# Moving the sample rows' top-k rounds from the delta stage back into the last projections

## The reference, cut to what matters

```python
# sparse attention: the indexer's score, and the keys that it leaves
score = jnp.einsum('bqh,bqhk->bqk', iw, jax.nn.relu(dots))     # 8 index heads
_, idx = lax.top_k(score, n_top)        # prompt 128 of 512 keys, sample rows 68 of 272
...
# delta rule, per chunk of 64: decay from cumulative gates, triangular solve, state
decay = jnp.exp(jnp.where(tri, gc[..., :, None] - gc[..., None, :], -jnp.inf))
sol = lax.linalg.triangular_solve(a, rhs, left_side=True, lower=True, unit_diagonal=True)
```

## Time and profile before

| | |
|---|---|
| median of 3 runs | 1534.19 us |
| the profiled execution's own time | 1533.19 us |
| its span, first to last instruction | 1531.4 us |
| PE busy | 1449.6 us, 95% |
| DVE busy | 883.3 us, 58% |
| mean granted TensorE clock | 0.977 |
| end of the projections, start of the delta stage | about 809 us into the span |

### The profile page before, as it was taken

One profiled execution on the slowest core, in us unless ns is written; L12 is line 12 of the kernel. 1 busy time (PEld: TensorE's weight loads), 2 busy tenths in 40 slices (PEclk: granted clock), 3 DMA queues, 4 the chain that ended last, 5 costly groups with the idle time before them and its releaser, 6 DMA issues. The chain is left out here.

```text
span 1531.4 us, 28524 instructions
## 1 busy us (share of the span) xinstructions
PE 1449.6 (95%) x11426; PEld 1351.3 (88%) x11430; DVE 883.3 (58%) x1637; ACT 573.9 (37%) x1130; POOL 394.7 (26%) x360
## 2 busy tenths in 40 slices
PE   6899999999999989998998889998999999999996
PEld 3889999999999989988896668688899999999995
DVE  2636665575477451576565766563557458754863
ACT  2632332342243252653324423542544124422443
POOL 1702420331242240541002030112723024302400
PEclk9899999999999989999999999999999999999998
DMA  9424445445443323222106020233113312331221
GB/s 344 130 83 139 152 132 172 138 145 165 131 139 100 96 57 78 78 69 62 50 1 160 2 88 16 71 100 87 56 42 97 97 56 84 96 98 48 83 77 69
DMA packets 211736, 148.76 MB, mean 97 GB/s; under 512 B 18075, under 2 KB 190396, under 8 KB 211608
## 3 DMA queue, kind: packets, MB, share of 16 engines
q1 hardware_dynamic: 206264, 129.15, 28.8%
q0 software_dynamic: 5344, 17.81, 3.7%
HBM read 139.99 MB, written 6.95 MB: 96 GB/s over the span
## 5 line engine op out<-in xcount | busy, mean ns | idle before, releaser
L1005 PE MATMUL pair<-b_hi,w_hi 128*128 128x320 f32 x720 | 224.3, 312 | 0.0
L1005 PE MATMUL pair<-b_hi,w_lo 128*128 128x320 f32 x720 | 222.5, 309 | 0.0
L1005 PE MATMUL pair<-b_lo,w_hi 128*128 128x320 f32 x720 | 222.4, 309 | 0.0
L1075 PE MATMUL pair<-act_hi,w_hi 128*128 128x320 f32 x704 | 161.9, 311 | 0.0
L1075 PE MATMUL pair<-act_hi,w_lo 128*128 128x320 f32 x704 | 160.4, 309 | 0.0
L1075 PE MATMUL pair<-act_lo,w_hi 128*128 128x320 f32 x704 | 160.4, 309 | 0.0
L471 DVE SCALAR_TENSOR_TENSOR x_t<-pair,gate,x_t 128x320 f32<-128x320 f32 (+1 forms) x128 | 56.0, 479 | 167.5 <-PE pair L1075 142.1
L1005 PEld LDWEIGHTS pair<-b_hi,w_hi 128*128 128x128 f32 x720 | 135.1, 188 | 14.3 <-DVE w_lo L594 8.4
L588 ACT ACTIVATE w_hi<-sums_a 128x512 fp32r<-128x512 f32 x72 | 45.1, 627 | 251.9 <-POOL sums_a L622 132.0
L890 DVE TENSOR_TENSOR uvw<-pair,uvw 128x320 f32<-128x320 f32 (+1 forms) x126 | 67.6, 537 | 123.1 <-PE pair L1005 122.7
L1005 PEld LDWEIGHTS pair<-b_lo,w_hi 128*128 128x128 f32 x720 | 135.2, 188 | 0.0
(11 more groups left out here) (428 smaller groups left out, 3160.2 us busy)
## 6 DMA issues: line engine op xcount, KB each, us to landing
w_mod_raw<-w_mod SPq DMA_DIRECT2D x28, 1024.0 KB, 6.0
w_raw<-ffn_w_gate SPq DMA_DIRECT2D x40, 512.0 KB, 4.1
raw_more<-ffn_w_up SPq DMA_DIRECT2D x40, 512.0 KB, 3.8
w_raw<-w_in SPq DMA_DIRECT2D x24, 512.0 KB, 3.7
w_raw<-ffn_w_down SPq DMA_DIRECT2D x16, 384.0 KB, 3.3
raw_more<-ffn_w_down SPq DMA_DIRECT2D x16, 384.0 KB, 3.1
w_mod_a<-w_mod POOLq DMA_DIRECT2D x4, 1024.0 KB, 10.9
w_mod_b<-w_mod POOLq DMA_DIRECT2D x4, 1024.0 KB, 24.1
```

Source lines behind the costliest of these rows:

```text
L1005: mm = pe.matmul(job_bank(j, BANK_OF[part]), w[:, at, kk], mv[:, kk, s], start=(kk == 0 and v == 0 and part in FIRST_OF_BANK), stop=(kk == ...
L1075: mm = pe.matmul(pair[part % 2][:, b, 0:HALF], w[:, slot, k], mv[:, k, b * HALF:(b + 1) * HALF], start=(k == 0 and v == 0), stop=(k == n - ...
```

## The change

The sample job becomes an ordinary fourth job of `next_rounds`. Its scores are copied at its first round, now into the score buffer. It may start once v is at least 25, so that it comes behind the third job: 6 rounds at the end of v = 28, and the last 2, the partial round and the mask at the end of v = 29. All calls of `sample_rounds` and `sample_mask` in the delta stage go. SP, ahead of the bias rows, and ACT, ahead of the first exponential, now wait for the fifth mask instead of the fourth. PE's waits are as they were.

```diff
@@ mix_loads (SP), and exps (ACT) with the same edit
-            sp.wait_ge(S["mask"], 4)
+            sp.wait_ge(S["mask"], 5)
@@ mix_dve
-            score_s = v_f[:, TOK - LS:]
...
+                first = left[job] == TOPK_S // 8
                 left[job] -= n
                 final = not left[job]
-                s = score_of(job)
+                s = score[:, SCORE_AT[job]:SCORE_AT[job] + SCORE_N[job]]
+                if job == 3 and first:
+                    dve.wait_ge(S["sscore"], NB)
+                    dve.tensor_copy(s, bank[3][:, 0:LS]).then_inc(S["sscore_out"], 1)
+                    dve.wait_ge(S["sscore_out"], 1)
                 topk(job, n, at)
-                if final and job < 3:
+                if job == 3 and final and TOPK_S % 8:
+
+                    link(dve.max(mx[:], s))
+                    link(dve.memset(mx[:, TOPK_S % 8:], NEG_TAKEN))
+                    link(dve.match_replace(s, mx[:], s, NEG_TAKEN))
+                if final:
                     make_mask(job)
...
-                if v >= SCORE_V + IDX_HEADS // PER_STEP and any(left[0:3]):
+                if v >= SCORE_V + IDX_HEADS // PER_STEP and (any(left[0:3]) or any(left) and v >= SAMPLE_V + NB // 2):
                     next_rounds(2 if v <= V["g", 11] else 1 if v <= V["aq", 1] else 6)
-            while any(left[0:3]):
+            while any(left):
                 next_rounds(4)
-            sample_scores()
@@ delta_dve, levels of the sample tile, and level 1
-                sample_rounds(1 if lv else 2)
...
-            sample_rounds(2)
-            level(1, 0, both((sample_rounds, 1), (w_out, 0)))
+            level(1, 0, lambda: w_out(0))
             level(1, 1, None, place_own)
-            level(1, 2, both((sample_mask,), (new_v, 0)))
+            level(1, 2, lambda: new_v(0))
```

More of the change, by code:

```diff
@@ L1765, in exps @@
                 if j == 0:
-                    act.wait_ge(S["mask"], 4)
+                    act.wait_ge(S["mask"], 5)
                     act.wait_ge(S["sscore"], NB)
@@ L1822, in mix_dve @@
             link = chained(dve, S["chain"])
-            score_s = v_f[:, TOK - LS:]
-            def score_of(job):
-                return score[:, SCORE_AT[job]:SCORE_AT[job] + SCORE_N[job]] if job < 3 else score_s
             def topk(job, n, before):
-                s = score_of(job)
+                s = score[:, SCORE_AT[job]:SCORE_AT[job] + SCORE_N[job]]
                 with dve.Fori(0, n) as i:
@@ L1856, in next_rounds @@
                 at = sum((ROUNDS,) * job) + (ROUNDS if job < 3 else TOPK_S // 8) - left[job]
+                first = left[job] == TOPK_S // 8
                 left[job] -= n
                 final = not left[job]
-                s = score_of(job)
-                topk(job, n, at)
-                if final and job < 3:
-                    make_mask(job)
[L1864 to L1875, removed]
+                s = score[:, SCORE_AT[job]:SCORE_AT[job] + SCORE_N[job]]
+                if job == 3 and first:
+                    dve.wait_ge(S["sscore"], NB)
+                    dve.tensor_copy(s, bank[3][:, 0:LS]).then_inc(S["sscore_out"], 1)
+                    dve.wait_ge(S["sscore_out"], 1)
+                topk(job, n, at)
+                if job == 3 and final and TOPK_S % 8:
[3 more added lines that the diff above has]
+                if final:
+                    make_mask(job)
             def place_v(h, part):
@@ L2003, in mix_dve @@
             dve.wait_ge(S["cols"], 1)
-            delta_dve(dve, link, next_rounds, sample_mask, *attention_dve(dve, link))
+            delta_dve(dve, link, *attention_dve(dve, link))
             dve.wait_ge(S["st_out"], 16)
@@ L2011, in mix_dve, with delta_dve @@
                 add_to_x(dve, 1, U_OUT + m, m, X_OUT + m, U_OUT + m + 2)
-        def delta_dve(dve, link, sample_rounds, sample_mask, biased, normed, place_own):
+        def delta_dve(dve, link, biased, normed, place_own):
             def matrices(q):
```

## The result

| | before | after |
|---|---|---|
| median, comparison of the change (6 runs each) | 1534.08 us (1533.19 to 1534.84) | 1543.19 us (1541.0 to 1546.8) |
| median, compared once more (`e1_again`) | 1535.05 us (30 runs, 1533.14 to 1541.12) | 1540.74 us (11 runs, 1538.35 to 1544.5) |
| the profiled execution: time, span, mean granted clock | 1533.19, 1531.4, 0.977 | 1539.34, 1537.5, 0.977 |

The change makes the kernel slower: the ratio is 1.006, with an interval of 1.0048 to 1.0073, and 1.004 (1.0027 to 1.0053) the second time. The sign and the place of the first delay are as forecast. The median of 1543.19 us is 4.5 us above the forecast of 1538.7, and 0.7 us above the end of its range; the second one, 1540.74 us, lies inside the range. Beside its six runs the first comparison has two more executions of the kernel after, of 1539.34 us (the profiled one) and 1543.66 us.

The account below looks back on a forecast made before the run. PE, busy for 95% of the span, was taken to bound the kernel. Terms 7.8 - 0.5 - 1.5 + 0.65 = 6.4 us, less 2.6 times about three quarters, gave 4.5 us: 1538.7 us forecast, range 1535.7 to 1542.5.

Parts of the forecast that it names:

- Steps 1 and 2: Border of projection and delta stage: DVE gets 13.65 us more, 5.64 us of cover, `matrices(0)` 7.8 us late at 818.9.
- Step 3: From `matrices(0)` to `k_in`: 0.60 us of waiting for PE falls away, `k_in` 7.3 us late at 822.3.
- step 4: First L2018 against POOL: up to 0.4 us more, none taken; 0 to 0.6 us kept for collisions with `matrices(1)`.
- Step 5: `k_in` to `matrices(1)`: 1.5 us saved by two rounds gone, 0.65 lost to a cold clock; transposes 6.4 us late.
- Step 6: Later levels: the removed rounds and mask give back nothing more, turning into longer waits for other engines.
- Step 7: First level's clock: back at 827.2 to 830.2, saving up to 2.6 us; delay at L2424 taken as 4.5 us.
- step 8: Bias rows behind the fifth mask: first group lands at 823.4, `biased(0)` may start as late as 825.5, costed at nothing.
- the delay stays to the end: Behind the first level all work follows PE, so the delay was taken to remain unchanged.
- worse: Rival: half clock through the first level and one more, or late bias rows; 9.0 us slower, 1543.2 us, chance 0.15.
- Absorbed: Rival: clock back before the first level's transposes, small savings come; 2.5 us slower, 1536.7 us, within 0.2%, chance 0.2.
- faster: Rival: each removed round was on the delta stage's path; 5.6 us faster, 1528.6 us, chance 0.06.

Follow-up runs that it names:

- e1_again: The changed kernel once more, without an edit: 1540.74 us, ratio 1.004 to the kernel before.
- e14_after_poolfar_busy: Changed kernel with unread products in PE's waits, POOL's sample scaling held until the first `k_in`, the prompts' until the first `w`: 1534.66 us, ratio 0.9986.
- e9_border5_busy: Kernel before with unread products in PE's waits, five sample rounds at the border and one in each of the next three levels: 1527.47 us, ratio 0.9949.
- e2_old_waits: Changed kernel with sample scores in the old place and SP and ACT waiting for the fourth mask as before: 1542.28 us, ratio 1.0043.
- e4_fit3: Kernel before with three sample rounds at the border, none in the first level, one each in the next three: 1534.79 us, ratio 0.9999.
- e11_no_rounds_busy: Kernel before with unread products in PE's waits, without the sample job's eight whole rounds (its mask isn't the reference's): 1527.79 us, ratio 0.9949.
- e15_fit3_poolfar_busy: e4_fit3 with unread products in PE's waits, POOL's sample scaling held until the first `k_in`, the prompts' until the first `w`: 1529.99 us, ratio 0.9953.
- e5_after_busy: Changed kernel with unread products in PE's waits, in the first level and five later ones: 1533.64 us, ratio 0.9982.
- the pair with fillers: e5_after_busy and e6_before_busy, the kernels after and before with unread products in PE's waits: 1533.64 and 1526.08 us.
- e13_before_poolfar_busy: Kernel before with unread products in PE's waits, POOL's sample scaling held until the first `k_in`, the prompts' until the first `w`: 1529.22 us, ratio 0.9947.
- e17_before_poolown_busy: Kernel before with unread products in PE's waits, POOL's sample scaling held until the first `k_in`, the prompts' until `own_rows`: 1527.74 us, ratio 0.9942.
- e6_before_busy: Kernel before with unread products in PE's waits, 14 ahead of job 0 and others in five later waits: 1526.08 us, ratio 0.9941.

## Why the prediction was right and wrong

**Steps 1 and 2** hold. DVE works without a pause until 818.5, and `matrices(0)` starts at 818.49 (818.9 foretold).

**Step 3** gave 7.3 us of delay at `k_in`; it was 8.2. The 0.60 us of waiting did fall away, but **step 4** took no cost for POOL. Measured, L2009 takes 1.22 us, L2025 1.04 and L2026 1.14. The last two took 0.42 and 0.43 in `e14_after_poolfar_busy`, so 1.3 us of hold are new there. Step 4 bounded `matrices(0)` and `matrices(1)`, and not the operations between them. That these two are held only with POOL's chain in this place is shown by `e14_after_poolfar_busy`. What holds them isn't: by the rows POOL only issues transfers then, and beside the same issues they took 0.42 us in `e9_border5_busy`. It isn't SP's loads of the bias rows either, for in `e2_old_waits`, where all of these are issued by 815.3, they took 1.05 and 1.15 us. (The Trainium skill, SBUF — State Buffer, section "SBUF: two separate sides", has the loser of the shared ports wait for the whole instruction of the other. The rows agree in kind. They go further in size: with POOL's four operations behind one another, `m_mat` took 2.06 and 2.07 us instead of 0.42, more than one POOL operation of about 1.04 us explains.)

**Step 5** credited 1.5 us for the two rounds ahead of `matrices(1)`. The mechanism is right and the credit was not there to take: `e4_fit3` and `e11_no_rounds_busy` take those rounds away and gain nothing, because POOL holds DVE in their place, and `e15_fit3_poolfar_busy`, with POOL elsewhere, gains 1.5. The time of 4.0 us plus 0.65 from `k_in` to `matrices(1)` measured 4.87, and 4.02 with the gap filled (`e5_after_busy`), so that the cold clock cost 0.85. The step's result was transposes 6.4 us late. They were 7.4 us late (830.40 against 823.00), and the new hold of 1.3 us at L2025 and L2026 is the largest part that the sum lacks. Without any clock the steps give 7.8 - 0.5 - 1.5 = 5.8 us, and the pair with fillers measures 6.5: 4.5 of border and 2.0 of POOL. So the border was priced 1.3 us too high and POOL 2.0 too low, and it is partly luck that the sum came so near. Part of the first error can be read in `e13_before_poolfar_busy`: with POOL away `k_in` waits 1.33 us for PE before the change, and not 0.60, so that more cover falls away.

**Step 6** is shown: the two levels behind the first are as long as before (8.76 us each after, 8.77 and 8.76 before), `matrices(2)` waits 1.62 us for the decay instead of 0.65, and the eight rounds left out gain nothing.

**Step 7** held within the first level: the clock came back at 828.4, ahead of the transposes, and the delay shrank from 7.4 to 4.8 us, where 4.5 was forecast. That these are so near is again partly luck: the cold cost of 2.6 us (20.98 - 18.40) fell away whole, where three quarters of it were credited, and this made up for most of the missing 1.0 us. **What failed** is the sentence behind step 8, "the delay stays to the end", which puts the clock behind the first level at nothing. The work comes 5 us later, and the later falls of the clock meet it at other places and in part last longer: one new dip of 3.4 us in the profiled executions (6.1 us at the end instead of 4.8), and in ten of nineteen executions a mean clock of 0.972 or less, where the kernel before has that in 15 of 89. The profile of `e2_old_waits`, at 0.972, shows a dip of 20.5 us. Within the first group the change costs 4.9 us (1539.75 against 1534.88), close to the 4.5 of the forecast; it is the share of the second group that brings the median to 1540.7 and 1543.2, as far as the times and mean clocks show. By the mean, a clock of 0.969 instead of 0.977 is an estimated 25 us more at 1.2 GHz (0.008 of 1540 us, and each us there counts half). With the gaps of PE filled, both kernels lose most of this spread, the credit of step 7 goes too, and the difference is 7.6 us.

The rival "worse" had the right size, 9.0 us and 1543.2, and the wrong place: the first levels run as it was forecast, and the second stay at low clock is at 900 to 921. The profile before did show a dip at 904.1 to 911.0 on PE's path; the prediction's windows ended at 856, and it priced no dip behind them.

**Step 8** is shown by `e2_old_waits`. `biased(0)` started at 823.81, straight behind `k_in`. Where `k_in` comes earlier the margin is gone: in `e14_after_poolfar_busy` `biased(0)` waits 1.10 us for the bias rows, until 823.66 (823.4 foretold), but `matrices(1)` behind it still waits 0.93 us for ACT, so that it costs nothing there either. "Absorbed" is refuted by the 6.5 us of the pair, "faster" by `e11_no_rounds_busy`.

**What stays open.** That a low mean clock in the second group of the kernel after is the same long dip as in `e2_old_waits` is an inference: none of those ten executions has a profile. Why the clock of one and the same program falls longer in some executions than in others isn't settled. `e17_before_poolown_busy`, 7.1 us shorter than before between 809 and 921, has a median 1.7 us above `e6_before_busy`'s in another session, but the same ratio, 0.9942 against 0.9941, and its profile is that of its slowest execution: that one lost 2.8 us between 700 and 809, in a dip at 718.9 to 725.7 that isn't there in `e6_before_busy`'s. The fillers of the delta stage leave the dip at 1061 to 1071 as it was.

## What to carry to other kernels

Work moved over a border is free up to the idle time that it finds there (three to five of these rounds, in 5.64 us of idle time and with the two rounds behind it gone). Beyond that it delays what stands behind it by its full length; count it against that cover before moving all of it. Where PE waits for short spells, price the clock for the whole kernel and not for the stage that is changed: a delay of 5 us moved the later dips and cost up to 4 us more, and a few products that nobody reads, put into those waits, gained 9 us, more than any order of the rounds. They gained nothing ahead of the second feed-forward part, so each gap has to be measured. When an instruction goes from in front of a wait, look at what another engine does in the time that comes free, here POOL's scaling.

## What the hardware showed that I had not expected

POOL's work on SBUF data holds not only DVE's operations with two inputs from SBUF: the norm, a TENSOR_SCALAR in fp32 with one, took 1.29 and 1.07 us beside it instead of 0.49, and 1.23 and 1.00 instead of 0.42. MAX8 and MATCH_REPLACE8 ran beside POOL's four operations at their usual 0.44 and 0.43 us.

A bf16 product of 512 columns that reads a finished mask and whose result nobody reads kept the granted clock at 1.00 through each wait of PE that was filled with it in `e6_before_busy`; 14 in the first wait and 34 in five others made the kernel 0.6% faster. (The Trainium skill, TensorE: Matmul & The Clock Gate, section "What's actually happening", says that activity releases the throttle and that the count of slow matmuls varies from run to run. Mean clocks of 0.969 to 0.977 in executions of one kernel agree with the second, and the gain from the products with the first.)
